# A three-branch encoder trunk on one core: the first group of units in two halves, one norm over four retention tiles, and attention values in another PSUM bank

## The chip, the cores and the metric

One core of a Trainium2 chip runs the whole program in one launch. The metric is device time in microseconds; less is better. All data are float32. TensorE (PE in the profile) multiplies and writes only to PSUM, eight banks of 128 partitions by 512 floats. ScalarE (ACT), VectorE (DVE) and GpSimd (POOL) do the elementwise work, SyncE (SP) issues the transfers. Each engine runs its own instructions in program order and waits on semaphores for the others.

## The reference: what is computed

Two layers over x of 512 positions by 1024 features. Each layer is (cut):

```python
h = rms_norm(x, norm_mix_g[l])
aq, ak, av, rq, rk, rv, rg, sz, sxbc, sdt = jnp.split(h @ w_in[l], offs, axis=-1)
ya = swa_sink_attention(aq, ak, av, attn_sinks[l], attn_bias)   # window of 128, 8 heads
yr = retention(rq, rk, rv, rg, ret_gn_g[l])                     # 4 heads of 128 values
ys = ssd_mixer(sz, sxbc, sdt, ...)    # conv of 4 taps and silu on sxbc, softplus on sdt
x = x + jnp.concatenate([ya, yr, ys], axis=-1) @ w_out[l]
h = rms_norm(x, norm_ffn_g[l])
x = x + conv_ffn(h, ffn_w_up[l], ffn_conv_w[l], ffn_conv_b[l], ffn_w_down[l])
```

and a last `rms_norm`. `retention` ends by dividing each head's 128 values by their root mean square (the mean is taken out of the values beforehand) and multiplying with a weight and with silu of the gate.

## The kernel before, in words

**Products.** Features lie on partitions, the 512 positions on the free axis. Weights come as a stream of packs of 128x512 (four 128x128 tiles) through four slots. For each pack SP loads `w_raw[slot]`, ACT writes the rounded `w_hi` (line 481), POOL the rest `w_lo` (line 378). An activation is split the same way, so that one 128x128 tile costs three matmuls of 512 columns: w_hi by h_hi, w_hi by h_lo ("high products"), w_lo by h_hi ("low products"), all issued from line 1048. A *unit* is 128 output features. The input projection has 28 units of 8 tiles: U0 to U3 and D4 to D27. Units 0, 1, 2, 3, 5 and 7 go through the convolution, 4 and 6 are the attention's key and value, 8 to 11 its queries, 12 to 19 the retention's q, k and v, 20 to 23 the SSD gate z, 24 to 27 the retention gate. The output projection is D28 to D51, in three parts of eight units of 4 tiles: part 0 (D28 on) takes the SSD branch, part 1 (D36 on) attention, part 2 (D44 on) retention. The FFN follows with long loops.

**Order.** A string SCHEDULE names the steps of a layer. Every engine walks it and does its own part of each step; so a step's place fixes the order on each engine's queue. D units alternate between two banks, `dense[0]` and `dense[1]`, and unit n waits until DVE has read unit n-2 (`evac`; line 796 for inputs, 787 for outputs). The other matmuls use six banks `M[0]` to `M[5]`. BANKS says which step uses which; `take(name, i, l)` makes PE wait until the previous user of the bank in the order of the string has been read (`m_free`).

**Start of a layer.** U0 to U3 share eight packs, a pack holding one tile of each. G0 to G3 do packs 0 to 3 for all four units. NORM sums the squares over partitions with a matmul by ones (line 1093; it waits for `ssq_added`, DVE lines 714 and 698), ACT makes rstd from it (Ln, line 442, and Exp, line 445). Then come U0 (packs 4 to 7, eight high and four low products), DT (16 small matmuls with `wdt_g`, which DVE makes in line 748), U1, U2, TT, U3, D4. DVE scales U0 to U3 by rstd and convolves each (lines 736 and 739).

**Around the attention.** RVn (retention value n, transposed by matmuls into M[5]) is read by ACT line 596. ASn are the scores of two chunks (banks 0, 1, 4; read by DVE line 910 and ACT line 580), AXn the softmax on DVE, ATn transposes the probabilities into banks 2 and 3 (read by ACT line 588), AVn multiplies them with the values into M[0], read by ACT (line 498) and then by DVE (line 943). On ACT the step D20 also holds silu of z (line 525) and a square (line 529), and the copy of RV3 stands after it. SN is the SSD branch's norm. RP rotates queries and keys (DVE lines 954 to 958), RA and RB are the retention's scores and values; RA0 waits for the last RP's result (`rot_done`).

**Retention norm.** RN0 squares tiles 0 and 1 (ACT line 608), sums them over partitions (PE), takes Ln (611) and Exp (615), then squares tiles 2 and 3 (619); RN1, after D39, does the rest for those. RXn on DVE scales tile n (line 991), multiplies by the gate (993), ACT makes m_hi (498), DVE m_lo (728). D44 needs tile k's m_lo before its k-th tile.

Of the kernel before, what the change touches and what calls it, by code (L numbers as in the profile page):

```python
# [19 lines left out]
D, S, P = 1024, 512, 128  # L20
KD = D // P
# [10 lines left out]
SLOTS = 4  # L32
# [6 lines left out]
GROUP = 4  # L39
U_Z, U_RG = (20, 21, 22, 23), (24, 25, 26, 27)  # L40
# [15 lines left out]
def segments():  # L56
# [19 lines left out]
N_PACKS = len(PACK_END)  # L76
# [12 lines left out]
def step_of(name):  # L89
# [13 lines left out]
def bank_uses():  # L103


    count, number = [0] * 6, {}
    for name in SCHEDULE + ["FNORM"]:
        head, idx = step_of(name)
        banks = (5,) if name == "FNORM" else BANKS.get(head, ())
# [61 lines left out]
def build(nc, a, out):  # L171
    f32, f32r = mybir.dt.float32, mybir.dt.float32r
    ALU, ACT, AX = mybir.AluOpType, mybir.ActivationFunctionType, mybir.AxisListType
    with ExitStack() as ctx:
# [19 lines left out]
        rs2 = (ssq, rstd)  # L194
# [68 lines left out]
        wdt_ready, dts_done, dt_in = sem("wdt_ready"), sem("dts_done"), sem("dt_in")  # L263
# [31 lines left out]
        def _(sp):  # L295
# [8 lines left out]
            sp.dma_start(wdt_raw[:, :], a["wdt"]).then_inc(c_loaded, 16)  # L304
# [68 lines left out]
        def _(pool):  # L373
# [20 lines left out]

            with pool.Fori(0, DEPTH) as l:
                at = 1
# [13 lines left out]
        def _(act):  # L410
# [28 lines left out]
            def rms(e, name, l):  # L439

                act.wait_ge(m_ready[5], ready(name, 0, l))
                nc.scalar.activation(rstd[:, :], M[5][:, :], ACT.Ln, scale=1.0 / D,
                                     bias=par["eps"][:, 0:1]).then_inc(m_free[5], 1)
                act.wait_ge(m_free[5], ready(name, 0, l) + 1)
# [26 lines left out]
            with act.Fori(0, DEPTH) as l:  # L471
# [18 lines left out]
                def conv_silu(n):  # L490
# [3 lines left out]
                    act.wait_ge(conv_summed, l * 6 + t + 1)  # L494
# [5 lines left out]
                for name in SCHEDULE:  # L500
# [5 lines left out]
                    elif step == "U":  # L506
                        if n:
                            hi_to(2 * GROUP + SLOTS - 1)
                        if n == GROUP - 1:
                            hi_to(2 * GROUP + SLOTS + 1)  # L510
                        conv_silu(n)
                    elif step == "D":
# [6 lines left out]
                        if n in U_CONV:  # L519
                            conv_silu(n)  # L520
# [26 lines left out]
                    elif step == "CM":  # L547
                        act.wait_ge(m_ready[5], ready(name, 1, l))
# [40 lines left out]
                    elif step == "AV":  # L589
                        act.wait_ge(m_ready[0], ready(name, 0, l))  # L590
                        for c in range(2):
                            src = M[0][:, 256 * c:256 * c + 256].rearrange("p (t q) -> p t q", t=4)
# [10 lines left out]
                    elif step == "RN":  # L603

                        if n == 0:
                            act.wait_ge(m_free[4], ready("RB3", 1, l) + 1)
                            for j in range(2):
                                nc.scalar.activation(sq[:, j, :], ry[:, j, :], ACT.Square).then_inc(r_sq, 1)
                        for j in range(2):
                            act.wait_ge(m_ready[j], ready(name, j, l))  # L610
                            nc.scalar.activation(rs2[j][:, :], M[j][:, :], ACT.Ln, scale=1.0 / P,
                                                 bias=par["eps"][:, 0:1]).then_inc(m_free[j], 1)
                        for j in range(2):
                            act.wait_ge(m_free[j], ready(name, j, l) + 1)
                            nc.scalar.activation(rs2[j][:, :], rs2[j][:, :], ACT.Exp, scale=-0.5)\
                                .then_inc(r_rs, 1)
                        if n == 0:
                            for j in range(2):
                                nc.scalar.activation(sq[:, j, :], ry[:, 2 + j, :], ACT.Square).then_inc(r_sq, 1)
# [42 lines left out]
        def _(dve):  # L662
# [19 lines left out]
            link(V.memset(wdt_g[:, :, :], 0.0))  # L682
# [38 lines left out]
            with dve.Fori(0, DEPTH) as l:  # L721
                base[0] = l * DVE_LINKS
                links[0] = 3
# [7 lines left out]
                def conv(n):  # L731
# [4 lines left out]
                    link(V.tensor_scalar(dst, pad[:, n % 2, 3:3 + S], taps[:, bass.ds(l * 30 + t * 5 + 3, 1)],  # L736
                                         taps[:, bass.ds(l * 30 + t * 5 + 4, 1)], ALU.mult, ALU.add))
                    for k in (2, 1, 0):
                        ins = V.scalar_tensor_tensor(  # L739
                            dst, pad[:, n % 2, k:k + S], taps[:, bass.ds(l * 30 + t * 5 + k, 1)],  # L740
                            dst, ALU.mult, ALU.add)
                        if k:
# [5 lines left out]
                V.tensor_tensor(wdt_g[:, :, 0:8],  # L748
                                wdt_raw[:, bass.ds(l * 64, 64)].rearrange("p (k h) -> p k h", h=8),
                                par["g"][:, bass.ds(l * 2 * KD, KD)].unsqueeze(2).broadcast_to([P, KD, 8]),  # L750
                                ALU.mult).then_inc(wdt_ready, 1)
                for name in SCHEDULE:
                    step, n = step_of(name)
                    if step == "U":
# [3 lines left out]
                        row = pad[:, n % 2, 3:3 + S]  # L758
# [46 lines left out]
                    elif step == "DT":  # L805
                        dve.wait_ge(m_ready[5], ready(name, 0, l))
# [25 lines left out]
                    elif step == "CM":  # L832
# [699 lines left out]
```

## Time and profile before

| | us |
|---|---|
| median of three runs | 1305.99 (1304.16 to 1306.04) |
| profiled execution, its own time | 1307.44 |
| its span, first to last instruction | 1305.6 |
| PE busy in it | 1277.4 (98%) |
| DVE, ACT, POOL busy | 615.3, 565.3, 588.8 |

Matmuls are pipelined: their durations in the profile overlap, and a matmul of 512 columns has a duration of 390 ns but starts 227 ns after the one before. So a loss on PE is read from the starts, or from the idle time in brackets at the end of a row of the timeline, with the engine, tile and line that ended it. The two layers lie 639 us apart; times of layer 0 are given where both look alike.

### The profile page before, as it was taken

The page shows a single profiled execution, that of the slowest core. Times are in us where ns is not written, and L with a number is a line of the kernel's source. Part 1 is how long each engine was busy: PE and PEld are TensorE (multiplying, and loading weights), DVE is VectorE, ACT ScalarE, POOL GpSimd, SP SyncE. Part 2 cuts the span into 40 slices and gives each one's busy share as a digit, 9 for nine tenths or more (in the row PEclk, how much of TensorE's full clock was granted, in tenths as well). Part 3 has the DMA queues.
Part 4 walks back from the last instruction along what each step waited for, and adds up shares of the span by engine and source line. Part 5 has one row for each costly group of instructions (what it writes and reads, how often), then busy time and mean ns, then how long its engine had stood idle before and what let it go on. Part 6 is the DMA issues. An engine that isn't in the chain of part 4 may idle for free.

```text
span 1305.6 us, 21212 instructions
## 1 busy us (share of the span) xinstructions
PE 1277.4 (98%) x6114; PEld 1032.3 (79%) x6114; DVE 615.3 (47%) x938; ACT 565.3 (43%) x902; POOL 588.8 (45%) x435
## 2 busy tenths in 40 slices
PE   7999999999999999999999999999999999999996
PEld 4888877778888888888878887777888888888885
DVE  6755666474444103332256556755653430133323
ACT  6432483465444223443344327726644332244433
POOL 4533434254444544554444443424455454455541
PEclk9999999999999999999999999999999999999998
DMA  7335212143333333333323432212333333333333
GB/s 221 91 111 137 74 56 74 49 112 90 96 96 96 97 97 97 96 96 90 98 89 89 131 106 73 76 47 67 91 111 98 96 101 97 91 96 97 96 95 113
DMA packets 77483, 125.29 MB, mean 96 GB/s; under 512 B 7752, under 2 KB 20456, under 8 KB 77288
## 3 DMA queue, kind: packets, MB, share of 16 engines
q1 hardware_dynamic: 77416, 124.43, 33.6%
q8 instruction: 38, 0.62, 0.2%
q14 instruction: 29, 0.24, 0.1%
HBM read 121.84 MB, written 2.55 MB: 95 GB/s over the span
## 4 chain that ended last, share of the span: by engine, by line
PE 83%; DVE 8%; ACT 4%; issue 4%; DMA 0%; DVEq 0%; SPq 0%; ACTq 0%
PE dense L1048 76%; PE mix L1048 6%; DVE h_lo L690 1%; ACT w_hi L481 1%; DVE arena L991 1%; DVE ssq L698 1%; DVE arena L739 1%; ACT L525 1%; DVE arena L993 1%; ACT m_hi L498 0%; DMA x<-in_xT 0%; DVE arena L910 0%; ACT pad L525 0%; DVE mx L920 0%; DVE arena L926 0%
## 5 line engine op out<-in xcount | busy, mean ns | idle before, releaser
L378 POOL TENSOR_TENSOR w_lo<-w_raw,w_hi 128x512 fp32r<-128x512 f32 x424 | 580.3, 1384 | 686.8 <-ACT w_hi L481 680.1
L1048 PE MATMUL dense<-h_hi,w_hi 128*128 128x512 f32 x1120 | 445.3, 398 | 3.9 <-DVE h_lo L690 3.0
L1048 PE MATMUL dense<-h_lo,w_hi 128*128 128x512 f32 x1120 | 437.3, 390 | 0.0
L481 ACT ACTIVATE w_hi<-w_raw 128x512 fp32r<-128x512 f32 x422 | 256.3, 627 | 258.4 <-PE dense L1048 242.4
L1048 PE MATMUL dense<-h_hi,w_lo 128*128 128x512 f32 x1120 | 300.5, 389 | 0.0
L1048 PEld LDWEIGHTS dense<-h_hi,w_hi 128*128 128x128 f32 x1120 | 211.0, 188 | 55.3 <-issue 10.0
L1048 PEld LDWEIGHTS dense<-h_lo,w_hi 128*128 128x128 f32 x1120 | 211.0, 188 | 45.2 <-issue 2.7
L1048 PEld LDWEIGHTS dense<-h_hi,w_lo 128*128 128x128 f32 x1120 | 210.4, 188 | 44.4
L1048 PE MATMUL dense<-m_hi,w_hi 128*128 128x512 f32 x544 | 217.3, 400 | 3.2 <-ACT w_hi L481 2.5
L1048 PE MATMUL dense<-m_lo,w_hi 128*128 128x512 f32 x544 | 212.0, 390 | 0.0
L1048 PE MATMUL dense<-m_hi,w_lo 128*128 128x512 f32 x544 | 146.9, 389 | 0.0
L1048 PEld LDWEIGHTS dense<-m_hi,w_hi 128*128 128x128 f32 x544 | 102.1, 188 | 28.9 <-DVE x L787 3.3
L1048 PEld LDWEIGHTS dense<-m_lo,w_hi 128*128 128x128 f32 x544 | 102.1, 188 | 23.0 <-issue 2.4
L1048 PEld LDWEIGHTS dense<-m_hi,w_lo 128*128 128x128 f32 x544 | 102.1, 188 | 21.4
L1029 DVE TENSOR_TENSOR x<-dense,x 128x512 f32<-128x512 f32 x32 | 22.1, 692 | 192.5 <-PE dense L1048 192.5
L1007 DVE TENSOR_TENSOR arena<-dense,rstd 128x512 f32<-128x512 f32 x44 | 30.5, 692 | 93.6 <-PE dense L1048 93.6
L641 ACT ACTIVATE arena<-arena 128x512 f32<-128x512 f32 x44 | 27.9, 634 | 85.9 <-DVE arena L1014 85.9
L1017 DVE TENSOR_TENSOR arena<-dense,rstd 128x512 f32<-128x512 f32 x44 | 30.4, 691 | 71.2 <-PE dense L1048 71.2
L1010 DVE SCALAR_TENSOR_TENSOR arena<-arena,params 128x512 f32<-128x512 f32 x44 | 35.7, 811 | 59.7 <-ACT arena L636 59.7
L1048 PE MATMUL mix<-arena 64*128 64x128 f32 (+4 forms) x696 | 56.6, 297 | 3.7 <-DVE arena L910 3.7
L423 ACT ACTIVATE h_hi<-x,params 128x512 fp32r<-128x512 f32 x39 | 28.3, 725 | 71.1 <-DVE x L1029 59.5
L1048 PEld LDWEIGHTS mix<-arena 128*64 128x64 f32 (+3 forms) x696 | 42.9, 160 | 17.1 <-issue 12.8
(173 smaller groups left out, 958.3 us busy)
## 6 DMA issues: line engine op xcount, KB each, us to landing
w_raw<-in_w SPq DMA_DIRECT2D x428, 256.0 KB, 2.6
arena<-cum_rows SPq DMA_DIRECT2D x8, 512.0 KB, 5.7
x<-in_xT SPq DMA_DIRECT2D x8, 256.0 KB, 6.3
out_y<-arena SPq DMA_DIRECT2D x8, 256.0 KB, 2.1
arena<-exp_rows SPq DMA_DIRECT2D x12, 128.0 KB, 6.4
consts<-in_consts SPq DMA_DIRECT2D x1, 1223.0 KB, 9.2
rel_scratch<-arena SPq DMA_DIRECT2D x1, 382.0 KB
bias<-rel_scratch SPq DMA_DIRECT2D x8, 32.0 KB, 2.5
```

The lines of the kernel that those rows point to most:

```text
L378: nc.gpsimd.tensor_tensor(w_lo[:, s, :], w_raw[:, s, :], w_hi[:, s, :].bitcast(f32), ALU.subtract).then_inc(lo_ready, 1)
L423: nc.scalar.activation(h_hi[:, o, :], x[:, o, :], ACT.Copy, scale=gcol(e, o)).then_inc(h_hi_ready, 1)
L481: nc.scalar.activation(w_hi[:, slot, :], w_raw[:, slot, :], ACT.Copy).then_inc(hi_ready, 1)
L525: nc.scalar.activation(zt, zt, ACT.Silu).then_inc(z_silu, 1)
L641: nc.scalar.activation(fs, fy, ACT.Silu).then_inc(f_silu, 1)
L690: V.scalar_tensor_tensor(h_lo[:, o, :], x[:, o, :], gcol(e, o), h_hi[:, o, :].bitcast(f32), ALU.mult, ALU.subtract).then_inc(h_lo_ready, 1)
L698: V.tensor_tensor(ssq[:, :], ssq[:, :], sq[:, o % 2, :], ALU.add).then_inc(ssq_added, 1)
L1007: V.tensor_tensor(fpad[:, 2:2 + S], dense[0][:, :], rstd[:, :], ALU.mult).then_inc(evac, 1)
L1010: ins = V.scalar_tensor_tensor(fy, fpad[:, 1:1 + S], par["fconv"][:, bass.ds(fi * 4 + 1, 1)], fy, ALU.mult, ALU.add)
L1017: V.tensor_tensor(fb, dense[1][:, :], rstd[:, :], ALU.mult).then_inc(evac, 1)
L1029: V.tensor_tensor(x[:, o, :], dense[n % 2][:, :], x[:, o, :], ALU.add).then_inc(evac, 1)
L1048: return T.matmul(dst, lhsT, rhs, start=start, stop=stop)
```

## The change

1. The string begins "G0 G1 G2 G3 H0 H1 NORM DT L0 U0 DX L1 U1 L2 L3 TT TK D4 U2 ...". H0 and H1 are the high products of U0 and U1 with packs 4 to 7, L0 and L1 their low products; L2 does both kinds for U2, L3 for U3 as before. NORM uses M[1], DT stays in M[5]. U0, U1, U2, U3 and DX are now steps of ACT and DVE alone: DX is DVE's reading of DT's result.
2. DVE and ACT take U2 after D4, and U3 after D6. CM's readings move ahead of D7 (ACT's CR before U3, DVE's CX behind it). The convolution's two row buffers alternate by CONV_ORDER. ACT's calls of `hi_to` (which packs' w_hi it makes at which step) follow.
3. `wdt_g` is zeroed and made by POOL instead of DVE; wdt has a semaphore of its own.
4. The retention norm squares all four tiles at RN0. RN0 sums tiles 0 and 1, RM0 (after D36) tiles 2 and 3, in banks 2 and 3; ACT does four Ln, then the w_hi of up to two packs, then four Exp. RX2 stands after D40, RX3 after D41.
5. AVn writes M[5] instead of M[0].

```diff
-    "G0 G1 G2 G3 NORM U0 DT U1 U2 TK U3 TT D4 DTB D5 DTC D6 D7 CM D8 BC TOL D9 SA0 ...
+    "G0 G1 G2 G3 H0 H1 NORM DT L0 U0 DX L1 U1 L2 L3 TT TK D4 U2 DTB D5 DTC D6 CR U3 CX D7 CM D8 BC TOL D9 SA0 ...
...
-    "RB0 RA1 D32 RB1 RA2 D33 RB2 RA3 D34 RB3 D35 RN0 D36 D37 RX0 D38 RX1 D39 RN1 D40 D41 RX2 D42 RX3 "
+    "RB0 RA1 D32 RB1 RA2 D33 RB2 RA3 D34 RB3 D35 RN0 D36 RM0 D37 RX0 D38 RX1 D39 D40 RX2 D41 RX3 D42 "
...
-    "NORM": (5,), "DT": (5,), ... "AV": (0,), "RP": (4,), "RV": (5,), ... "RN": (0, 1),
+    "NORM": (1,), "DT": (5,), ... "AV": (5,), "RP": (4,), "RV": (5,), ... "RN": (0, 1), "RM": (2, 3),
...
+            nc.gpsimd.memset(wdt_g[:, :, :], 0.0).then_inc(wdt_zero, 1)
+            pool.wait_ge(p_loaded, 16)
+            pool.wait_ge(wdt_loaded, 16)
+            pool.wait_ge(wdt_zero, 1)
             with pool.Fori(0, DEPTH) as l:
+                nc.gpsimd.tensor_tensor(wdt_g[:, :, 0:8], wdt_raw..., par["g"]..., ALU.mult).then_inc(wdt_ready, 1)
...
-                        if n:
-                            hi_to(2 * GROUP + SLOTS - 1)
-                        if n == GROUP - 1:
-                            hi_to(2 * GROUP + SLOTS + 1)
+                            hi_to({1: 11, 2: 13, 3: 19}[n])
...
                         if n in U_CONV:
+                            hi_to(2 * n + 7)
                             conv_silu(n)
...
+                        act.wait_ge(m_free[4], ready("RB3", 1, l) + 1)
+                        for t in range(4):
+                            nc.scalar.activation(sq4[t], ry[:, t, :], ACT.Square).then_inc(r_sq, 1)
+                    elif step == "RM":
+                        where = [("RN0", 0), ("RN0", 1), ("RM0", 0), ("RM0", 1)]
+                        for t, (name, i) in enumerate(where):
+                            act.wait_ge(m_ready[t], ready(name, i, l))
+                            nc.scalar.activation(rs4[t], M[t][:, :], ACT.Ln, ...).then_inc(m_free[t], 1)
+                        hi_to(packs[0] + 1)
+                        for t, (name, i) in enumerate(where):
+                            act.wait_ge(m_free[t], ready(name, i, l) + 1)
+                            nc.scalar.activation(rs4[t], rs4[t], ACT.Exp, scale=-0.5).then_inc(r_rs, 1)
...
+                def group_high(u):
+                    for k in range(SLOTS, KD):
+                        h_tile(l * 2)(k)
+                        pe.wait_ge(hi_ready, l * N_PACKS + k + 1)
+                        group_mm(u, k, False)
+                def group_low(u):
+                    for k in range(SLOTS, KD):
+                        pe.wait_ge(lo_ready, l * N_PACKS + k + 1 + SLOTS)
+                        ins = group_mm(u, k, True, stop=k == KD - 1)
+                    ins.then_inc(run_done, 1)
...
-                                ins = mm(M[0][r, 256 * c:256 * c + 256], vwin[:, n % 2, c, r],
+                                ins = mm(M[5][r, 256 * c:256 * c + 256], vwin[:, n % 2, c, r],
```

## Rows read from the trace of the kernel before

**Rows 1.** The page, chain that ended last, shares of the span by engine

```profile
PE 83%; DVE 8%; ACT 4%; issue 4%; DMA 0%; DVEq 0%; SPq 0%; ACTq 0%
```

**Rows 2.** What PE waited for: us in total, times, longest us

```profile
PE mix L1048 <- DVE arena L910: 3.7, 2, 1.8
PE mix L1048 <- DVE ssq L698: 3.4, 1, 3.4
...
PE dense L1048 <- ACT w_hi L481: 2.5, 2, 1.3
```

**Rows 3.** The chain in order of time: start us, us, what

```profile
299.25 353.63 PE dense L1048 x1560
```

**Rows 4.** Timeline, PE, start of each layer: start us, us, instruction [idle before]

```profile
20.03 0.63 PE L1048 MATMUL mix<-h_hi,w_lo 128*128 128x512 f32 x2
...
24.02 1.77 PE L1048 MATMUL mix<-ssq,consts 128*128 128x512 f32 x2 [3.36 <-DVE ssq L698]
...
40.43 0.49 PE L1048 MATMUL dense<-h_hi,w_hi 128*128 128x512 f32 x1
...
664.24 1.02 PE L1048 MATMUL mix<-ssq,consts 128*128 128x512 f32 x2
...
678.93 0.49 PE L1048 MATMUL dense<-h_hi,w_hi 128*128 128x512 f32 x1
```

**Rows 5.** Timeline, DVE and ACT, start of layer 0

```profile
20.57 3.31 DVE L698 TENSOR_TENSOR ssq<-ssq,sq 128x512 f32<-128x512 f32 x2
...
22.02 0.63 ACT L481 ACTIVATE w_hi<-w_raw 128x512 fp32r<-128x512 f32 x1 [0.74 <-DMA w_raw<-in_w]
```

**Rows 6.** Busy time by stretch: bounds, length, each engine, PE clock, DMA share, GB/s

```profile
24.36:27.80 3.44, 3.44 (x8) 2.09 (x7) 0.73 (x1) 1.96 (x2) 1.88 (x2) 0.50 0.54 86
...
182.00:186.50 4.50, 2.66 (x16) 1.40 (x14) 4.46 (x5) 2.97 (x5) 0.93 (x1) 1.00 0.02 9
```

**Rows 7.** Timeline, PE: RV3 and AV0 of layer 0

```profile
151.93 1.05 PE L1048 MATMUL mix<-consts,pad 128*128 128x128 f32 x8
...
152.91 1.08 PE L1048 MATMUL mix<-arena 128*64 128x256 f32 x8
```

**Rows 8.** Timeline, ACT: the copy of RV3 in both layers

```profile
157.27 0.58 ACT L596 ACTIVATE arena<-mix 128x512 f32<-128x512 f32 x1
...
796.57 0.58 ACT L596 ACTIVATE arena<-mix 128x512 f32<-128x512 f32 x1
```

**Rows 9.** Timeline, ACT, PE, DVE: AV2 of layer 0, two rotations, RA0

```profile
182.35 1.07 ACT L588 ACTIVATE arena<-mix 128x512 f32<-128x512 f32 x2
...
184.81 1.08 PE L1048 MATMUL mix<-arena 128*64 128x256 f32 x8 [1.84 <-DVE arena L910]
...
210.90 0.69 DVE L954 TENSOR_TENSOR ssq<-mix,consts 128x512 f32<-128x512 f32 x1 [0.24 <-PE mix L1048]
...
216.24 0.69 DVE L958 TENSOR_TENSOR arena<-arena,ssq 128x512 f32<-128x512 f32 x1
...
217.07 0.43 PE L1302 MATMUL mix<-consts,arena 128*128 128x128 f32 x2
```

**Rows 10.** Timeline, PE, retention norm of layer 0

```profile
243.06 1.88 PE L1048 MATMUL mix<-sq,consts 128*128 128x512 f32 x4
...
264.32 0.47 PE L1048 MATMUL dense<-m_hi,w_hi 128*128 128x512 f32 x1 [1.26 <-ACT w_hi L481]
...
271.73 0.50 PE L1048 MATMUL dense<-m_hi,w_hi 128*128 128x512 f32 x1 [0.33 <-DVE m_lo L728]
```

**Rows 11.** Timeline, ACT and DVE, retention norm of layer 0

```profile
251.06 1.80 DVE L991 SCALAR_TENSOR_TENSOR arena<-arena,params,ssq 128x512 f32<-128x512 f32 x1
...
261.21 1.28 ACT L615 ACT_TABLE_LOAD   x1
...
263.71 0.74 DVE L991 SCALAR_TENSOR_TENSOR arena<-arena,params,ssq 128x512 f32<-128x512 f32 x1
```

**Rows 12.** Timeline, POOL, beside the first of those DVE rows

```profile
249.78 2.54 POOL L378 TENSOR_TENSOR w_lo<-w_raw,w_hi 128x512 fp32r<-128x512 f32 x2 [6.92 <-ACT w_hi L481]
```

More of the change, by code:

```diff
@@ L108, in bank_uses @@
         head, idx = step_of(name)
-        banks = (5,) if name == "FNORM" else BANKS.get(head, ())
+        banks = BANKS["NORM"] if name == "FNORM" else BANKS.get(head, ())
         for i, b in enumerate(banks):
@@ L193, in build @@
         rot = rs = ssq
-        rs2 = (ssq, rstd)
+        rs4 = (ssq[:, :], rstd[:, :], sq[:, 0, :], sq[:, 1, :])
+        sq4 = (sq[:, 0, :], sq[:, 1, :], pad[:, 0, 4:4 + S], pad[:, 1, 4:4 + S])
         c_all, p_all = sb("consts", [P, sum(CONSTS.values())]), sb("params", [P, sum(PARAMS.values())])
@@ L439, in rms @@
             def rms(e, name, l):
[L441 to L444, printed above, removed]
+                act.wait_ge(m_ready[1], ready(name, 0, l))
+                nc.scalar.activation(rstd[:, :], M[1][:, :], ACT.Ln, scale=1.0 / D,
+                                     bias=par["eps"][:, 0:1]).then_inc(m_free[1], 1)
+                act.wait_ge(m_free[1], ready(name, 0, l) + 1)
                 nc.scalar.activation(rstd[:, :], rstd[:, :], ACT.Exp, scale=-0.5).then_inc(rstd_ready, 1)
@@ L546, in _ @@
                         nc.scalar.activation(dt_u[:, :], dt_u[:, :], ACT.Ln).then_inc(dt_ln, 1)
-                    elif step == "CM":
-                        act.wait_ge(m_ready[5], ready(name, 1, l))
+                    elif step == "CR":
+                        hi_to(19)
+                        act.wait_ge(m_ready[5], ready("CM", 1, l))
                         nc.scalar.activation(crows[:, 0, :], M[5][:, 0:P], ACT.Copy).then_inc(rows_done, 1)
@@ L603, in _ @@
                     elif step == "RN":
[L605 to L619, printed above, removed]
+                        act.wait_ge(m_free[4], ready("RB3", 1, l) + 1)
[5 more added lines that the diff above has]
+                            act.wait_ge(m_ready[t], ready(name, i, l))
+                            nc.scalar.activation(rs4[t], M[t][:, :], ACT.Ln, scale=1.0 / P,
+                                                 bias=par["eps"][:, 0:1]).then_inc(m_free[t], 1)
+                        hi_to(packs[0] + 1)
+                        for t, (name, i) in enumerate(where):
+                            act.wait_ge(m_free[t], ready(name, i, l) + 1)
+                            nc.scalar.activation(rs4[t], rs4[t], ACT.Exp, scale=-0.5).then_inc(r_rs, 1)
                     elif step == "RX":
@@ L757, in _ @@
                         dve.wait_ge(run_done, l * N_SEGS + (SEG0 + UNIT_END[n]))
-                        row = pad[:, n % 2, 3:3 + S]
+                        row = pad[:, CONV_ORDER.index(n) % 2, 3:3 + S]
                         if n < 2:
@@ L804, in _ @@
                             V.tensor_tensor(xs[:, t, :], xs[:, t, :], row, ALU.mult).then_inc(yg_done, 1)
-                    elif step == "DT":
-                        dve.wait_ge(m_ready[5], ready(name, 0, l))
+                    elif step == "DX":
+                        dve.wait_ge(m_ready[5], ready("DT", 0, l))
                         V.tensor_tensor(dts, M[5][:, :], rstd[:, :], ALU.mult).then_inc(m_free[5], 1)
@@ L831, in _ @@
                                                ALU.mult, ALU.mult).then_inc(dt_done, 1)
-                    elif step == "CM":
-                        dve.wait_ge(m_ready[4], ready(name, 0, l))
+                    elif step == "CX":
+                        dve.wait_ge(m_ready[4], ready("CM", 0, l))
                         link(V.tensor_copy(tok[:, 32:64], M[4][:, 0:32]))
                         V.tensor_copy(lastb[:, :], M[4][:, 32:64]).then_inc(m_free[4], 1)
-                        dve.wait_ge(m_free[4], ready(name, 0, l) + 1)
+                        dve.wait_ge(m_free[4], ready("CM", 0, l) + 1)
                         V.tensor_tensor(wdec[:, :], lastb[:, :], tok[:, 32:64], ALU.subtract).then_inc(wdec_in, 1)
@@ L1133, in group_unit, with group_last @@
                         group_mm(u, k, False)
[L1134 to L1140 removed]
+                def group_low(u):
[3 more added lines that the diff above has]
+                    ins.then_inc(run_done, 1)
+                def group_last(u):
+                    for k in range(SLOTS, KD):
+                        group_mm(u, k, False)
+                        group_mm(u, k, True, stop=k == KD - 1).then_inc(run_done, 1)
                 def ret_tile(k):
@@ L1150, in _ @@
                         group_pack(n)
-                    elif step == "U":
-                        group_unit(n)
+                    elif step == "H":
+                        group_high(n)
+                    elif step == "L":
+                        if n == GROUP - 1:
+                            group_last(n)
+                        else:
+                            if n == GROUP - 2:
+                                group_high(n)
+                            group_low(n)
                     elif step == "D":
@@ L1160, in _ @@
                             elif n == N_IN + 8:
-                                pe.wait_ge(m_free[0], ready("AV3", 0, l) + 1)
+                                pe.wait_ge(m_free[5], ready("AV3", 0, l) + 1)
                             dense_unit(n, m_src(4 * part), ret_tile if n == N_IN + 16 else None)
@@ L1338, in _ @@
                             ins.then_inc(m_ready[5], 1)
-                    elif step == "RN":
+                    elif step in ("RN", "RM"):
                         for j in range(2):
-                            pe.wait_ge(r_sq, l * 4 + 2 * n + j + 1)
+                            t = j if step == "RN" else 2 + j
+                            pe.wait_ge(r_sq, l * 4 + t + 1)
                             take(name, j, l)
-                            mm(M[j][:, :], ones[:, :], sq[:, j, :]).then_inc(m_ready[j], 1)
+                            mm(M[t][:, :], ones[:, :], sq4[t]).then_inc(m_ready[t], 1)
                 for half, (g0, ng) in enumerate(HALVES):
```

55 lines of the change are left out of this document (24 added, 31 removed), and 8 rows, old and new, of tables (BANKS, SCHEDULE).

## Prediction

> **What bounds the kernel now.** First the page: PE is busy 98% of the span, and the chain that ended last lies 83% on PE, 12% on DVE and ACT [rows 1]. So only three things count: what PE executes, the moments in which it stands still, and its clock. The change leaves every matmul in, so the second and third decide. Next the list of PE's waits: 3.7 us in two waits for DVE's reading of scores (line 910), 3.4 us once for the sum of squares, 2.5 us in two for w_hi [rows 2]. The reader is to see how little there is to win: under 10 us of waits in the places that this change touches, so that one new wait of some microseconds in each layer can eat it all. The chain gives the pitch: 1560 products in 353.63 us, 0.227 us each [rows 3]. A dense unit of twelve products takes 2.72 us.
>
> **Start of a layer, edits 1 to 3.** In layer 0 the last of G3's low products start at 20.03 and are through at 20.49; NORM starts at 24.02, held by the sum of squares, and D4 at 40.43 [rows 4]. In layer 1 nothing holds NORM: from it to D4 are 678.93 - 664.24 = 14.69 us [rows 4]. Layer 0 took 16.41, that is 1.7 more, and the stretches say why: from 24.36 to 27.80 the granted clock was 0.50, 1.2 instead of 2.4 GHz, after PE had stood still [rows 6].
> New order in layer 0: H0's first six products take 1.36 us, to 21.85; the last two need pack 7's w_hi, ready at 22.02 + 0.63 = 22.65 [rows 5]; then 2 + 8 products, 2.27 us, to 24.9. The sum of squares is there at 20.57 + 3.31 = 23.88 [rows 5], so NORM doesn't wait. From NORM to D4 remain 14.69 less the 16 products that are already done (3.63): 11.06, D4 at 36.0 instead of 40.43. That is **4.4 us** gained, if a pause of 0.8 us leaves the clock alone; if not, 1.7 less. In layer 1 the products only change places: **0**.
> What is moved lies beside PE. rstd comes some 2.4 us later against PE's place in layer 1, but DVE and ACT have four D units (22 us) until the six convolutions are wanted (by SA0), and D6 and D7 need only the readings of D4 and D5, which now stand ahead of the convolutions of U2 and U3. POOL's small operation (64 columns; the bound is one w_lo, 1.3 us) falls where POOL waits for pack 4; it would cost only if low product 7 came after L0, and there are 3 us between. The rows of CM are read no later than before, so SP's transfers behind them aren't late either. I take 0 for all of this, and keep a loss of 1 us per layer as its bad end.
>
> **Attention values in M[5], edit 5: what it adds.** Bank users wait in the order of the string, and that is "RV3 AX1 AV0": AV0 now needs M[5], which RV3 has just filled. RV3 starts on PE at 151.93 and AV0 at 152.91 [rows 7]. But ACT copies RV3 out only at 157.27 to 157.85 [rows 8], behind the D20 step's table load, silu, the wait for DVE's product and the square. Nothing in that chain waits for AV0, and nothing in it gets shorter. So AV0 starts at about 157.97 (0.12 us of signalling, as between DVE's first reading of scores and AV2): PE stands for **5.06 us**. Layer 1 has the copy at 796.57, 639.30 later, in the same place [rows 8]: twice. Behind AV0 in PE's queue are D21, AT1 and AS2; DVE and ACT have next the reading of D21, silu and the reading of AS2's scores, and wait for PE too, so the loss is passed on almost whole. Before, DVE read D21 a little late, since AV0's reading stood ahead of it; after this stall it doesn't, which I put at 0.4 us of slack.
> The clock: the one long stall of the trace (3.5 us) was followed by half clock, 3.4 us of it, price 1.7 [rows 4, 6]; the stall of 1.84 was not, the stretch from 182.00 to 186.50 has clock 1.00 [rows 6]. A stall of 5.06 is beyond both. Part of the half-clock stretch may fall into the stall itself, so I take **1.2** each time, bounds 0 and 1.9.
> The Trainium skill (TensorE: Matmul & The Clock Gate, Part 1) says that an idle array drops to half its clock and that activity brings it back. The trace agrees at 24.36. A clock that never falls would make the sum 2.4 us smaller; it is a rival below.
>
> **Edit 5: what it removes.** AV2 waited for M[0] until DVE had read AS3's scores, 1.84 us [rows 9]. In M[5] it needs only ACT's two copies of AT2, done at 183.42 [rows 9], the first of them in time for its first half; so up to 1.84 go. But further on PE meets the rotations: the last one ends at 216.24 + 0.69 = 216.93 and RA0 starts at 217.07 [rows 9]. PE can't be earlier than that chain. It has slack of 0.14, three waits for PE of 0.24 like the one at 210.90 [rows 9], and the 0.4 from D21: 1.26 in all. I take **1.2** per layer, bounds 0.14 and 1.84.
>
> **Retention norm, edit 4.** Two waits on PE go, for a pack behind RN1's Ln and Exp (1.26) and for RX3's m_lo (0.33), 1.6 us idle and up to 1.9 from start to start [rows 10]. Now the new schedule. RN0 starts at 243.06, two sums cost 1.72 with their transition, D36 2.72, RM0 1.72: the fourth sum is there at 249.2. Ln 0.7, two packs 1.1, table load 1.28 [rows 11], Exp 0.63 like a pack's w_hi [rows 5]: RX0 can start at 253.1, against 251.06 before. Each RX takes 0.74 for line 991 [rows 11], 0.7 each for line 993, ACT's m_hi and m_lo, 2.8 with the gaps, and 0.6 for the reading of the D unit behind it. RX0 253.1, RX1 256.5, RX2 after D40's reading 261.0. Line 991 reads SBUF twice and took 1.80 instead of 0.74 where POOL's two w_lo of 2.54 us ran until 252.32 [rows 11, 12]: it ended 0.54 after them. That will strike RX2 (packs 69 and 70) and RX3 (pack 71), together 1.3. RX3 then ends near 268.4, D42's reading behind it at 269.0. PE without stalls is at D44 at 243.06 + 2 x 1.72 + 8 x 2.72 = 268.3 and needs that reading: 0.8 us of new stall. Gain 1.9 + 0.3 (slack in the starts) - 0.8, so **1.4** per layer; bounds 0 and 1.9.
> The Trainium skill (SBUF — State Buffer, Who interferes with whom) has the shared port pair of VectorE and GpSimd as an exclusive lock, held for an instruction; the 1.80 us agree. Without it the stall at D44 would be gone, and each layer 0.8 better.
>
> **Sum.** -4.4 (layer 0's start) + 2 x 5.06 (AV0) + 2 x 1.2 (clock) - 2 x 1.2 (AV2) - 2 x 1.4 (norm) = +2.9. Against the profiled execution's own 1307.44 (span 1305.6, 1.8 around it) that is 1310.3. It is 1.45 above the median, so against the median of 1305.99: **1308.9**.
>
> **Rivals.** About 0.2%, 2.6 us, is what a measurement of this kernel tells from no change.
> A, forecast (0.42): as above, the new wait outweighs all the rest.
> B, the clock stays at full rate, or the gains are at their upper ends (0.25): 1308.9 - 2.4 = 1306.5, no change. For it: when a fall sets in, one case can't tell. Against: the 3.5 us stall was enough.
> C, the other side (0.10): AV0 hardly waits, since RV3's copy comes much earlier on ACT in the new order. Then -4.4 - 2.4 - 2.8 = -9.6, 1296.4. It decides once wait and clock cost under 3.5 us per layer. Against it: ACT's D20 step is untouched, and its chain starts with AS1's scores, which follow PE.
> D, the retention norm gains nothing (0.13): all four Exp ahead of RX0, RX3 late, D44 waits 2.5 us instead of 0.8: +1.5 a layer, 1311.9. For it: five handovers in a row, each of which POOL can hold up. Against: RX0 ran under such a lock before, too [rows 11, 12].
> E, DVE is late after the first group (0.10): convolutions under the lock cost 1.6 us per tap; if U3's and D7's push silu past SA0, PE waits there, 1 to 3 us a layer, 1311 to 1315. Against: by my count silu of unit 7 is ready 3 us ahead of SA0.
>
> **Numbers.** Likeliest: 1308.9. All terms at their good ends give about 1302, at their bad ends 1316. C alone lies under 1302, D and E reach to 1315; leaving C out and most of E's far half, the range is 1303.5 to 1313.5. Faster by over 0.2%: C and a little of B, 0.12. Within 0.2%: the rest of B and the lower third of A, 0.38. Slower: 0.50.
>
> **What the new profile would show.** Layer 0: no idle before NORM, clock 1.0 in the first 40 us, D4 near 36.0. At AV0 a PE idle of about 5 us ended by ACT line 596's copy, in both layers, then a stretch at clock 0.5. No idle at AV2 behind DVE's scores; RA0 waiting for the last rotation. No idle at D40; at D44 one of under 1 us, ended by DVE. I'm wrong if AV0 starts right behind RV3, if the clock stays at 1.0 after it, or if PE waits anywhere between D4 and AS0.

## The result, and the profile after

| | before | after |
|---|---|---|
| median of the timed executions | 1305.86 us (1304.16 to 1306.04, 4) | 1313.53 us (1313.48 to 1313.86, 4) |
| profiled execution, its own time | 1307.44 | 1313.48 |
| its span | 1305.6 | 1311.6 |
| mean granted clock of PE | 0.996 | 0.992 |

The ratio is 1.0062, 95% interval 1.0045 to 1.008: slower by 0.6%, 7.7 us by the medians. The forecast was 1308.9, 2.9 us slower, with a range of 1303.5 to 1313.5. The direction was right, the size was not: the time is 4.6 us above the forecast and lies just outside the range.

Where it is lost shows at once in the list of what PE waited for in the changed kernel (us in total, times, longest us; the first rows). It answers to [rows 2]:

```profile
PE mix L1052 <- ACT arena L606: 10.0, 2, 5.0
PE dense L1052 <- DMA arena<-in_rel: 3.4, 1, 3.4
PE dense L1052 <- DVE h_lo L697: 3.1, 3, 2.6
PE mix L1052 <- DVE dt_a L832: 1.4, 2, 0.7
PE dense L1052 <- DVE x L791: 0.9, 2, 0.5
PE mix L1052 <- ACT arena L598: 0.7, 2, 0.3
PE dense L1052 <- ACT w_hi L491: 0.6, 2, 0.3
```

The waits for scores (3.7 us) and for the sum of squares (3.4) are gone. A new one of 10.0 us stands in their place: line 606 is ACT's copy of RV3. The two rows below it, for `in_rel` and `h_lo`, lie ahead of the first group and were there before with 3.3 and 3.0. The others are smaller new ones: for `dt_a`, for a reading of x at D44, for the copies of AT, for a pack at D11. Now the same places in the timeline of the changed kernel, PE (answers to [rows 4, 7, 9, 10]):

```profile
23.47 1.02 PE L1052 MATMUL mix<-ssq,consts 128*128 128x512 f32 x2
...
57.26 0.63 PE L1052 MATMUL mix<-dt_a,consts 128*128 128x32 f32 x4 [0.72 <-DVE dt_a L832]
...
77.31 0.47 PE L1052 MATMUL dense<-h_hi,w_hi 128*128 128x512 f32 x1 [0.28 <-ACT w_hi L491]
...
147.54 1.05 PE L1052 MATMUL mix<-consts,pad 128*128 128x128 f32 x8
153.59 1.98 PE L1052 MATMUL mix<-arena 128*64 128x256 f32 x8 [5.00 <-ACT arena L606]
...
185.54 1.14 PE L1052 MATMUL mix<-arena 128*64 128x256 f32 x8
...
218.67 0.43 PE L1319 MATMUL mix<-consts,arena 128*128 128x128 f32 x2
...
270.69 0.50 PE L1052 MATMUL dense<-m_hi,w_hi 128*128 128x512 f32 x1 [0.45 <-DVE x L791]
...
679.17 0.49 PE L1052 MATMUL dense<-h_hi,w_hi 128*128 128x512 f32 x1
...
798.32 1.98 PE L1052 MATMUL mix<-arena 128*64 128x256 f32 x8 [5.00 <-ACT arena L606]
```

NORM follows its predecessor without a pause; AV0 waits 5.00 in both layers; AV2, at 185.54, doesn't wait any more. ACT's queue ahead of the copy is as the prediction read it (timeline, ACT, layer 0):

```profile
149.54 1.28 ACT L534 ACT_TABLE_LOAD   x1
150.84 0.63 ACT L534 ACTIVATE pad<-pad 128x512 f32<-128x512 f32 x1
152.34 0.63 ACT L538 ACTIVATE sq<-arena 128x512 f32<-128x512 f32 x1 [0.88 <-DVE arena L808]
152.88 0.58 ACT L606 ACTIVATE arena<-mix 128x512 f32<-128x512 f32 x1
```

And the granted clock by stretch (bounds, length, busy PE, PEld, DVE, ACT, POOL, clock, DMA share, GB/s), which answers to [rows 6]:

```profile
20.00:36.00 16.00, 16.00 (x82) 11.63 (x81) 10.06 (x13) 8.53 (x11) 7.93 (x7) 1.00 0.50 112
151.10:157.93 6.83, 4.34 (x14) 2.76 (x15) 4.29 (x7) 2.15 (x5) 2.34 (x2) 0.50 0.48 143
158.00:164.00 6.00, 6.00 (x41) 5.00 (x42) 0.79 (x2) 1.90 (x3) 2.16 (x2) 1.00 0.13 44
182.00:187.00 5.00, 5.00 (x25) 3.32 (x24) 4.64 (x6) 4.16 (x8) 2.18 (x2) 1.00 0.38 105
796.20:803.10 6.90, 4.78 (x15) 3.11 (x16) 4.29 (x7) 1.78 (x5) 1.97 (x2) 0.51 0.42 126
```

From 20.00 to 36.00, which holds NORM and all up to D4, the clock is full. By 151.10, 2.5 us into the wait at AV0, it is down to 0.50 (1.2 instead of 2.4 GHz), and 4.34 us of busy time are spent at that level. A product starts every 0.43 us there instead of 0.227, so 4.34 x (1 - 0.227/0.43) = 2.0 us are lost.

The start of each step in the changed kernel's trace less its start in the trace before is this (PE, us; a negative number is earlier): D4 of layer 0 -5.95; RV3 -4.39; AV0 +0.68; RA0 +1.60; RN0 +1.58; FNORM (the FFN's norm) +0.33; layer 1's D4 +0.24, RV3 +1.05, AV0 +6.11, RA0 +7.21, FNORM +5.96, the end +5.95. Three things differ from the forecast: 1.56 of the gain is lost again between D4 and RV3, where nothing should have been lost (0.8 in layer 1); AV0 to RA0 cost 0.9 (1.1 in layer 1) where 0 was forecast (clock +1.2, AV2 -1.2); and the profiled pair differs by 6.0 us, the medians by 7.7.

### The profile page after: what moved, and what is told of

It reads as the page before. It is cut to its first block, busy times and chain, and to the rows that moved or that the text cites. A ratio compares the mean times of both kernels' runs of the same rounds, so it can differ in the third digit from the quotient of the medians.

```text
span 1311.6 us, 21171 instructions
## 1 busy us (share of the span) xinstructions
PE 1280.4 (98%) x6114; PEld 1033.7 (79%) x6114; DVE 623.1 (48%) x935; ACT 565.7 (43%) x902; POOL 587.7 (45%) x438
## 4 chain that ended last, share of the span: by engine, by line
PE 80%; DVE 10%; ACT 5%; issue 4%; DVEq 0%; DMA 0%; ACTq 0%; SPq 0%
PE dense L1052 72%; PE mix L1052 7%; DVE h_lo L697 2%; DVE arena L747 1%; ACT w_hi L491 1%; ACT m_hi L508 1%; ACT L534 1%; DVE mx L924 1%; DVE arena L930 1%; DVE arena L914 1%; DVE arena L744 0%; DVE ssq L705 0%; DVE arena L995 0%; DVE x L791 0%; ACT L543 0%
```

## The experiments

A run is compared with runs of the kernel before on the same chip; the medians of that one were 1304.74, 1305.66, 1305.71 and 1305.39 us in the four groups of runs. The code is cut to the lines that carry an edit; "..." marks what is left out.

### First group: the edits one by one

**av_only**: the kernel before with edit 5.

```diff
-    ... "AT": (2, 3), "AV": (0,), ...
+    ... "AT": (2, 3), "AV": (5,), ...
```


> The kernel before with edit 5 alone. Theory: two waits of 5.06 us for RV3's copy, two stretches at half clock that cost 1.91 and 2.10 us, and 1.99 us back between AV2 and RA0: 10.1 + 4.0 - 2.0 = +12.1, about 1318.0 against 1305.9. Rival: the price of the half clock was overlapped by the wait itself and costs nothing of its own: +8.1, 1314.0. Second rival: the wait is this long only because edits 1 to 3 shift the attention; alone it is under 2 us and the time stays below 1311.

Measured: 1317.08 us, ratio 1.0091 (1.0077 to 1.0104), +12.3. PE's row at AV0 in its timeline:

```profile
156.47 1.97 PE L1048 MATMUL mix<-arena 128*64 128x256 f32 x8 [4.93 <-ACT arena L596]
```

The wait is as long without the other edits (4.93 against 5.00), so it belongs to this edit alone. The time is that of the theory, and both rivals fall.

**av_back**: all but edit 5.

```diff
-    ... "AT": (2, 3), "AV": (5,), ...
+    ... "AT": (2, 3), "AV": (0,), ...
```


> The changed kernel with edit 5 undone (attention values in M[0] again), edits 1 to 4 kept. Theory: edit 5 is worth +12.1 here too, so 1313.5 - 12.1 = 1301.4; PE starts AV0 right behind RV3, no half clock there, and AV2 waits some 1.8 us for DVE's reading of scores again. Rival, that the edits hide each other (AV2's wait longer by what was saved): 1303 to 1305.

Measured: 1301.51 us, ratio 0.9977 (0.9968 to 0.9986). The change without edit 5 is faster than the kernel before, as the theory said. AV2 waits 1.82 us again.

**norm_only**: the kernel before with edit 4.

```diff
-    ... D35 RN0 D36 D37 RX0 D38 RX1 D39 RN1 D40 D41 RX2 D42 RX3
+    ... D35 RN0 D36 RM0 D37 RX0 D38 RX1 D39 D40 RX2 D41 RX3 D42
```


> The kernel before with edit 4 alone (retention norm of four tiles). Theory: from RN0 to FNORM the changed kernel took 1.25 and 1.24 us less; alone -2.5, 1303.4. Rival: the saving depends on the other edits' shift of ACT and POOL, then within 1 us of 1305.9.

Measured: 1301.88 us, ratio 0.998 (0.9971 to 0.9989), -2.9. The saving stands by itself; the rival falls.

**group_only**: the kernel before with edits 1 to 3.

```diff
-    "G0 G1 G2 G3 NORM U0 DT U1 U2 TK U3 TT D4 DTB D5 DTC D6 D7 CM D8 ...
+    "G0 G1 G2 G3 H0 H1 NORM DT L0 U0 DX L1 U1 L2 L3 TT TK D4 U2 DTB D5 DTC D6 CR U3 CX D7 CM D8 ...
```


> The kernel before with edits 1 to 3 alone. Theory: 5.95 us gained up to D4 of layer 0, 1.56 lost again up to RV3, 0.6 lost in layer 1: -3.8 against the profiled execution of before. But that one was 1.5 above the median of the timed runs, and I take it that its half-clock stretch at layer 0's start (1.7 us) is missing in most executions: then the medians differ by -2.2, 1303.7. Rival: the half-clock stretch is in every execution, and the medians differ by -3.8, 1302.1.

Measured: 1304.06 us, ratio 0.9993 (0.9983 to 1.0003): 0.7 us, not told from nothing, and less than theory and rival said; the theory's 2.2 us lie at the end of the interval. The largest gain of the forecast, 4.4 us, isn't there. The traces of this group give the first half of the reason; the fourth group gives the other. NORM and the clock behind it in norm_only, whose start of layer 0 is that of the kernel before (timeline PE; then a stretch):

```profile
22.32 1.12 PE L1047 MATMUL mix<-ssq,consts 128*128 128x512 f32 x2 [2.29 <-DVE ssq L697]
...
22.50:26.00 3.50, 3.50 (x14) 2.37 (x14) 0.89 (x1) 2.49 (x3) 2.06 (x2) 1.00 0.51 83
```

The same in av_only, with the same start:

```profile
22.63 1.12 PE L1048 MATMUL mix<-ssq,consts 128*128 128x512 f32 x2 [3.04 <-DVE ssq L698]
...
23.00:27.00 4.00, 4.00 (x11) 2.90 (x10) 0.70 (x1) 3.17 (x4) 1.86 (x2) 0.61 0.56 85
```

So the start that [rows 4, 6] show is not what every execution has. NORM came at 24.02, 22.63 and 22.32 and D4 at 40.43, 38.97 and 37.14, the last with the full clock. The changed start has D4 at 34.48, 34.56 and 34.77 in the traces of after, av_back and group_only. Against 37.14 that is 2.4 to 2.7 us and not 5.95. In the later traces with this start D4 lies between 34.05 and 35.39, so over all of them the gain is 1.8 to 3.1 us, against the one start at full clock.

### Second group: the wait at AV0, its clock, and ways around it

**filler**: products that nobody reads keep PE busy during the wait.

```diff
                     elif step == "AV":
+                        if n == 0:
+                            pe.wait_ge(evac, l * N_EV + 20)
+                            for _ in range(21):
+                                mm(dense[1][:, :], h_hi[:, 0, 0:P], h_hi[:, 0, :])
                         take(name, 0, l)
```


> The changed kernel with 21 products of 512 columns into dense[1] ahead of AV0, whose result nobody reads (D21 overwrites it); they take 21 x 0.227 = 4.8 us, so PE is busy during its wait for RV3's copy, which is as long as before. Theory: the half clock behind AV0 is due to the idle time; it goes, and with it 1.91 + 2.10 us: 1313.5 - 4.0 = 1309.5, AV0 at the same place. Rival: the clock falls for another reason (the 64-column products of AV0, or a power limit); then nothing changes, 1313.5.

Measured: 1309.36 us, ratio 1.0027 (1.0016 to 1.0037). AV0 and two stretches that hold the waits of both layers:

```profile
154.25 1.08 PE L1052 MATMUL mix<-arena 128*64 128x256 f32 x8 [0.31 <-ACT arena L606]
...
146.00:160.00 14.00, 13.69 (x69) 10.82 (x68) 5.75 (x9) 7.67 (x13) 6.47 (x5) 1.00 0.25 76
...
790.00:804.00 14.00, 13.70 (x70) 10.84 (x69) 5.17 (x9) 7.40 (x13) 6.79 (x5) 1.00 0.28 76
```

AV0 waits for the same copy, but PE worked meanwhile and the clock stays at 1.00: it is the idle time that brings the fall, and the rival (the products of AV0 themselves, or power) is out. The time falls by 4.2 us against 1313.53 and by 3.9 against the changed kernel's later run. That is the price of the two half-clock stretches, shown apart from the wait.

**rv_first**: ACT copies RV3 ahead of the D20 step's table load.

```diff
+                        if n == 20:
+                            act.wait_ge(m_ready[5], ready("RV3", 0, l))
+                            nc.scalar.activation(vtok[:, :, 3, :], bank(5, 4), ACT.Copy).then_inc(m_free[5], 1)
                         if n in U_CONV:
...
-                    elif step == "RV":
+                    elif step == "RV" and n < 3:
```


> The changed kernel with ACT's copy of RV3 moved ahead of the table load and silu of the D20 step. Theory: the copy stands at 149.6 to 150.2 instead of 152.88 to 153.46 and AV0 starts at 150.3, a wait of 1.7 us instead of 5.07; that is -3.3 per layer, and the clock stays full, as it did behind the wait of 1.84: -2.0 more. Together 1313.5 - 10.6 = 1302.9. Rival: the clock falls behind 1.7 us of idle time as well: 1306.9. Second rival: silu of the gate comes 0.6 us later and DVE's later work hands that on to RA0: 1304.

Measured: 1302.72 us, ratio 0.998 (0.9971 to 0.9989), as expected. The waits list has

```profile
PE mix L1055 <- ACT arena L529: 3.1, 2, 1.5
```

Line 529 is the copy in its new place. Only that place changed, 10.8 us went, and behind these waits of 1.5 us the clock stayed full. The length of the wait is set by what stands ahead of the copy in ACT's queue.

**av_split**: AV0 in M[0], AV1 to AV3 in M[5].

```diff
-    ... "AT": (2, 3), "AV": (5,), ...
+    ... "AT": (2, 3), "AV0": (0,), "AV": (5,), ...
```


> The changed kernel with the first attention values (AV0) in M[0] as before, AV1 to AV3 in M[5]. Theory: no wait at AV0 and none at AV2; against the kernel with all four in M[0] (1301.5) each layer gains the 1.0 us that the changed kernel kept of AV2's 1.85: 1299.5. Rival: without the stall at AV0 the rotations end as late as in before, RA0 waits for them and only 0.3 us a layer stays: 1300.9.

Measured: 1300.24 us, ratio 0.9956 (0.9943 to 0.997), between theory and rival. The list names 0.2 us in each layer at RA0, behind the last rotation:

```profile
PE mix L1321 <- DVE arena L964: 0.4, 2, 0.2
```

Without AV0's stall RA0 does meet the rotations, and 1.3 us of the two times 1.85 remain by the medians of av_back and av_split; in their traces AV1 to RA0 is 0.57 us shorter in each layer.

**split_dtc_hi**: av_split with two moves between D4 and SA0.

```diff
-    ... TT TK D4 U2 DTB D5 DTC D6 CR ...
+    ... TT TK D4 U2 DTB DTC D5 D6 CR ...
...
                     elif step == "SA":
+                        if n == 0:
+                            hi_to(23)
```


> As av_split, and besides DTC stands ahead of D5 in the string (DVE makes dt_a before D5's convolution instead of behind it) and ACT makes the rounded packs 22 and 23 ahead of SA0's exponentials. Theory: CM's wait for dt_a (0.72 a layer) and D11's for pack 22 (0.44) both go, 1.2 a layer: 1297.1. Rival: DVE is the bound between D4 and SA0, and the wait comes back at D8 for the reading of D6, or at SA0: under 0.5 us in all, 1299.

Measured: 1297.52 us, ratio 0.9936 (0.9923 to 0.995). It is the fastest version found, 8 us ahead of the kernel before. Its trace has no wait of PE from 40 to 90 us nor from 700 to 735.

### Third group: before's executions, and which part of edits 1 to 3 costs

**after_again**: the changed kernel once more.


> The changed kernel as it is, once more, beside the others. Theory: its own time scatters little (1313.5 to 1313.9 so far), while the kernel before falls into two groups near 1304.2 and 1305.9; the difference is 7.6 to 9 us by the share of the two groups. Rival: it scatters as much as before does.

Measured: 1313.27 us (1312.84 to 1316.31), ratio 1.0067 (1.0055 to 1.0079), +7.6: the loss is there again. Its scatter, 3.5 us in six executions, is not as small as the theory had it.

**before_fill**: the kernel before, with products that nobody reads in layer 0's wait for the sum of squares.

```diff
                     elif step == "NORM":
+                        with pe.If(l < 1):
+                            take("TK", 0, l)
+                            for _ in range(12):
+                                mm(M[4][:, :], h_hi[:, 0, 0:P], h_hi[:, 0, :])
                         norm(l * 2, name, l)
```


> The kernel before with 12 products of 512 columns (2.72 us) into the idle bank M[4] ahead of layer 0's NORM, in its wait for the sum of squares; nobody reads their result. Theory: the group of executions near 1305.9 is that with half clock behind this wait; with PE busy it is gone, and all but a stray run lie near 1304.2, with D4 14.7 us behind NORM. Rival: the two groups come from elsewhere (loads, the stall at AV2); then they stay, median 1304.2 to 1305.9.

Measured: 1304.79 us, ratio 0.9996 (0.9987 to 1.0005). Of eleven executions eight had the mean clock 0.997 and times of 1304.18 to 1305.54, three 0.996 and 1305.67 to 1306.25. The profiled one is of the second kind. Its rows at NORM and at AV2 of layer 1, and the stretches:

```profile
22.54 1.12 PE L1048 MATMUL mix<-ssq,consts 128*128 128x512 f32 x2 [0.58 <-DVE ssq L698]
...
820.75 1.08 PE L1048 MATMUL mix<-arena 128*64 128x256 f32 x8 [1.82 <-DVE arena L910]
...
20.00:26.00 6.00, 5.42 (x22) 3.85 (x21) 3.58 (x5) 4.07 (x5) 4.79 (x4) 1.00 0.54 80
820.00:826.00 6.00, 5.25 (x18) 3.19 (x19) 5.13 (x9) 2.85 (x5) 0.05 (x1) 0.72 0.00 0
```

The start is free of the half clock, as the theory said. But here it fell behind the stall of 1.82 at AV2, which the forecast, by [rows 6], had taken to be too short for it. The trace of norm_only has the same in layer 1:

```profile
819.19 1.08 PE L1047 MATMUL mix<-arena 128*64 128x256 f32 x8 [1.82 <-DVE arena L909]
...
819.00:826.00 7.00, 6.81 (x24) 4.47 (x25) 6.03 (x11) 3.83 (x6) 1.62 (x2) 0.76 0.00 0
```

Theory and rival are each right in part: a stall at either place brings the fall in some executions. The six traces with all attention values in M[0] hold twelve stalls of 1.8 us at AV2, and these two alone were followed by half clock; from AV2 to AV3 it cost 1.6 us each time. The interval of the ratio holds 1, so what the fall at the start costs a typical execution is not shown by this run.

**split_dtc**: av_split with DTC moved alone.

```diff
-    ... TT TK D4 U2 DTB D5 DTC D6 CR ...
+    ... TT TK D4 U2 DTB DTC D5 D6 CR ...
```


> AV0 in M[0] and DTC ahead of D5, without the earlier packs 22 and 23. Theory: of the 2.7 us between 1300.2 and 1297.5, CM's wait for dt_a is 0.9 per layer, pack 22 0.5: 1298.5. Rival: once dt_a is earlier the rest of the chain to SA0's exponentials is too and pack 22 comes in time by itself: 1297.5, as both together.

Measured: 1301.45 us, ratio 0.997 (0.9959 to 0.9982): 1.2 us slower than av_split, which neither theory expected. In its waits the one for `dt_a` is gone, and one for `w_hi` has grown:

```profile
PE dense L1054 <- ACT w_hi L491: 3.4, 2, 1.7
```

DVE's timeline in it shows both sides of the move:

```profile
49.81 0.19 DVE L831 SCALAR_TENSOR_TENSOR dt_w<-dt_u,dt_w 128x32 f32<-128x32 f32 x1 [1.31 <-ACT dt_u L555]
50.04 0.19 DVE L832 TENSOR_TENSOR tok<-dt_a,dt_w 128x32 f32<-128x32 f32 x1
50.27 0.19 DVE L833 SCALAR_TENSOR_TENSOR dt_a<-tok,exp_a 128x32 f32<-128x32 f32 x1
```

The three small operations cost 0.19 each: they run just before POOL begins its next products. But DVE idles 1.31 us for the logarithm first, its convolutions end later, SA0's exponentials too, and pack 22 is rounded behind them. PE, which no longer waits at CM, stands at D11 instead.

**order_back**: av_split with edit 2 undone. In it the convolution of unit 5 reads the other of the two row buffers than D5's reading has filled, so its values are not the reference's; the operations are as many and as large. Besides the order, ACT makes the packs from 14 on as late as before.

```diff
-    ... L1 U1 L2 L3 TT TK D4 U2 DTB D5 DTC D6 CR U3 CX D7 CM D8 ...
+    ... L1 U1 L2 L3 U2 TT TK U3 D4 DTB D5 DTC D6 D7 CM CR CX D8 ...
```


> AV0 in M[0], edits 1, 3, 4 kept, but edit 2 undone: DVE and ACT take U2 and U3 ahead of D4 as before, CM's readings stand behind D7, ACT makes the packs from 14 on as late as before. Theory: POOL's row of five products under dt_a is gone with the early packs, so the waits for dt_a and for pack 22 (1.3 us a layer) go: 1297.7. Rival: the loss is the price of edit 1, PE being 6 us further ahead of DVE in layer 0: DVE then does four convolutions before D4's reading, and PE waits at CM or SA0 at least as long as with edit 2: 1300.2 or more.

Measured: 1309.35 us, ratio 1.0034 (1.0021 to 1.0047), 9 us slower than av_split. The theory falls, though its first half came true: POOL stood idle when DVE made `dt_a`, whose three operations took 0.19 each, and there is no wait for `dt_a`. The rival holds in its size, not in its place. With U3's convolution ahead of D4's reading PE waits for that reading, at D6:

```profile
50.22 0.50 PE L1052 MATMUL dense<-h_hi,w_hi 128*128 128x512 f32 x1 [3.87 <-DVE arena L799]
```

Layer 1 has 3.85. The clock fell behind both (0.69 from 50.20 to 54.00), about 1 us more in each layer. Edit 2 is what makes edit 1 bearable: between D4 and SA0 it is DVE that PE runs into.

### Fourth group: what is lost between D4 and RV3

**split_hi**: av_split with the packs alone.

```diff
                     elif step == "SA":
+                        if n == 0:
+                            hi_to(23)
```


> AV0 in M[0] and packs 22 and 23 rounded ahead of SA0's exponentials; DTC behind D5's convolution as in the changed kernel. Theory: the wait at D11 (0.3 to 0.5 us a layer) goes, the wait for dt_a (0.7 to 0.9) stays: 1300.2 - 0.8 = 1299.4, between av_split and the kernel with both moves (1297.5). Rival: the late pack is the only loss there is and the wait for dt_a is made up on the way: 1297.5.

Measured: 1299.28 us, ratio 0.9953 (0.9939 to 0.9966); the theory's 1299.4. In its trace D4 to RV3 is 0.53 and 0.52 us shorter than in av_split's; the wait for `dt_a` (0.7) is still there.

**group_dtc_hi**: group_only with both moves.

```diff
-    ... TT TK D4 U2 DTB D5 DTC D6 CR ...
+    ... TT TK D4 U2 DTB DTC D5 D6 CR ...
...
                     elif step == "SA":
+                        if n == 0:
+                            hi_to(23)
```


> The kernel before with edits 1 to 3 and both moves (DTC ahead of D5, packs 22 and 23 ahead of SA0's exponentials), without edits 4 and 5. Theory: edits 1 to 3 gained little (0.7 us) because two new waits between D4 and RV3 took 1.3 us a layer back; without these the gain is whole: 1304.1 - 2.7 = 1301.4 against 1304.7 of before. Rival: the gain of edits 1 to 3 is small for another reason, and the two moves bring as much only with edits 4 and 5: 1303 or more.

Measured: 1301.1 us, ratio 0.9969 (0.9956 to 0.9981), -4.3 where group_only had -0.7. Its trace shows no wait for `dt_a` or pack 22, and what it has gained at D4 of layer 0 it still has at RV3: 111.47 us between them, 113.01 in group_only, 111.50 before. The two late handovers were the loss of edits 1 to 3.

## Why the prediction was right or wrong

**The wait at AV0, 2 x 5.06.** Right to a hundredth: from RV3 to AV0 0.98 us before, 6.05 after, 5.07 more, in both layers. av_only, av_back and rv_first show it as a matter of bank order and ACT's queue alone. Rival C is out.

**The clock, 2 x 1.2.** The mechanism was right; filler shows it. The size was not: 3.9 to 4.2 us in time for both layers. In the trace AV0 to AV1 grew by 1.9 and 2.1 us, at and above the upper bound of 1.9. The forecast let part of the half-clock stretch fall into the stall itself. In fact 2.5 of the 6.83 us at half clock lay in the stall, and the clock was granted again only 4.34 us after PE had taken up work. Rival B is out.

**AV2, 2 x (-1.2).** AV2 doesn't wait any more, but the changed kernel kept 1.0 per layer of the 1.85. Small delays took the rest before RA0: AV3 for the copies of AT 0.4 from start to start, the second rotation's product for DVE's reading of the first 0.3, D27 for a pack 0.1. The forecast was 0.2 too much per layer.

**Retention norm, 2 x (-1.4).** 1.25 and 1.24 in the traces, 2.9 in the time of norm_only. The new wait forecast at D44 with 0.8 us is there, ended by DVE, with 0.45. Rival D is out.

**Layer 0's start, -4.4, and "I take 0 for all of this".** This is the step that failed, in two ways.
First, the size of the start. D4 was forecast at 36.0 and came at 34.48: 0.65 us because G3 ended earlier in this execution (H0 starts at 19.84, not 20.49), 0.8 because pack 7's high part was ready at 20.68 and H0 ran through. But the start before, D4 at 40.43, is not typical. Of the 73 executions of the kernel before in the four groups 30 have a mean clock of 0.997, with a median of 1304.2 us; the other 43, with 0.993 to 0.996, have 1306.0. The profiled one, with 0.996 and 1307.44, is slower than 68 of them: of the traces seen it had the longest wait, and the half clock. Its 1.7 us of half clock were counted as a gain in the -4.4, and then the sum was moved down by 1.45 from that execution to the median, which takes off much the same peculiarity a second time. Against the one traced start at full clock the gain at D4 is 2.4 to 2.7 us, 1.8 to 3.1 over all traces.
Second, the handovers: PE does wait between D4 and AS0, at CM and at D11, which the prediction had put at 0 and had named as a sign of being wrong. Rival E's mechanism came, in a milder form and elsewhere than looked for. The first five rows show how DVE and POOL stand before CM in the kernel before, the other four the same in the changed kernel (timelines):

```profile
58.13 0.18 DVE L826 SCALAR_TENSOR_TENSOR dt_w<-dt_u,dt_w 128x32 f32<-128x32 f32 x1
58.35 0.20 DVE L827 TENSOR_TENSOR tok<-dt_a,dt_w 128x32 f32<-128x32 f32 x1
58.58 0.19 DVE L828 SCALAR_TENSOR_TENSOR dt_a<-tok,exp_a 128x32 f32<-128x32 f32 x1
...
53.14 2.73 POOL L378 TENSOR_TENSOR w_lo<-w_raw,w_hi 128x512 fp32r<-128x512 f32 x2 [1.66 <-ACT w_hi L481]
59.49 5.05 POOL L378 TENSOR_TENSOR w_lo<-w_raw,w_hi 128x512 fp32r<-128x512 f32 x4 [3.61 <-ACT w_hi L481]
...
53.37 1.28 DVE L830 SCALAR_TENSOR_TENSOR dt_w<-dt_u,dt_w 128x32 f32<-128x32 f32 x1
54.68 1.21 DVE L831 TENSOR_TENSOR tok<-dt_a,dt_w 128x32 f32<-128x32 f32 x1
55.93 1.20 DVE L832 SCALAR_TENSOR_TENSOR dt_a<-tok,exp_a 128x32 f32<-128x32 f32 x1
...
49.40 7.68 POOL L380 TENSOR_TENSOR w_lo<-w_raw,w_hi 128x512 fp32r<-128x512 f32 x5 [3.36 <-ACT w_hi L491]
```

Before, POOL was idle from 55.87 to 59.49 and the three operations fell into that. Edit 2's calls of `hi_to` give POOL five products in a row from 49.40 to 57.08. DVE's three operations of 32 columns take 1.2 us each beside them instead of 0.19, and CM waits 0.72. The Trainium skill (SBUF — State Buffer, Who interferes with whom) has the port pair of VectorE and GpSimd as an exclusive lock; these rows agree: three operations that read two tiles of SBUF pay 1.0 to 1.1 us each beside POOL's products, as much as the 1.06 of the full-width operation in [rows 11]. The forecast had counted this price for the norm's full-width operations only. The second handover is pack 22 behind SA0's exponentials (at 77.31, and in layer 1). Together 1.56 us in layer 0 and 0.8 in layer 1. Taking both away brings 3.0 us in time, from group_only (1304.06) to group_dtc_hi (1301.1), and 1.54 and 1.48 in their traces: in layer 1 that is 0.7 more than the edits had cost, since the kernel before itself takes 0.8 us longer from D4 to RV3 there than in layer 0.

**Sum.** The forecast was +2.9, the medians say +7.7. Layer 0's start and the handovers: -0.7 measured where -4.4 was forecast, 3.7 of the error. The clock: 3.9 instead of 2.4, 1.5 of it. The rest is under 0.5 each. Measured one by one the edits give -0.7 (1 to 3), -2.9 (4) and +12.3 (5), together +8.7, one more than the whole change; each carries an interval of over 1 us.
The prediction's ends of the sum don't come out of its own bounds: at their good ends its terms (start -4.4, wait 10.1, clock 0, AV2 2 x -1.84, norm 2 x -1.9) give 1304.2, not 1302, at their bad ends (start -2.7, a loss of 2, wait 10.1, clock 3.8, AV2 -0.3, norm 0) 1318.9, not 1316.

**Open.** Why the same stall is followed by half clock in one execution and not in the next isn't settled; that it happens at NORM (in two of three traces of the untouched start) and at AV2 (two of twelve stalls) is seen, but that is too few for shares. How much of group_only's small gain is a different share of such executions can't be told from its eleven.

## What to carry to other kernels

Before a step gets another bank, find the step that holds it and where its reader stands in the reader's queue: 5 us of table load, silu, a wait for DVE and a square ahead of one copy outweighed all other gains, and leaving one of four steps in its old bank turned +7.7 into -5.4 us. Ask of the profiled execution whether it is typical (mean clock, time against the median) before a stall or a slow stretch of it is booked as a gain. When PE is sent ahead, move its suppliers' small operations and packs forward too, both together: one alone only moved the wait.

## What the runs showed of the hardware

The clock's fall behind a stall is not fixed by the stall's length: behind 1.84 us it stayed at 1.00 [rows 6], behind 1.82 at the same step of layer 1 in before_fill it was 0.72 over 820 to 826; behind 2.29 it stayed, behind 3.04 it fell, and behind 3.87 and 3.85 in order_back too. Behind all six waits of 4.9 to 5.0 (after, after_again, av_only) it fell. In filler, where PE had other work in that wait, it stayed at 1.00. A fall at AV0 cost 1.5 to 2.2 us (AV0 to AV1 took 15.96 to 16.72 us against 14.49 in filler), and products that nobody reads won back 3.9 us over two such stalls.

A DVE operation on 32 columns that reads two tiles of SBUF took 0.18 to 0.20 us with POOL idle (before, split_dtc, order_back) and 1.20 to 1.28 beside POOL's products of 1.54 us (after).
